# The RWKV scan of a hybrid backbone, laid out by parity of the channel tile: 64x64 products on four TensorE quadrants, key products a chunk further ahead

## The chip, the cores and the metric

The kernel runs on one core of one Trainium2 chip. The metric is device time in microseconds, the median of several runs. TensorE (PE) multiplies, with the stationary operand loaded first (PEld); VectorE (DVE), ScalarE (ACT) and GpSimd (POOL) move and combine data; SyncE (SP) issues DMAs. The TensorE array has 128 input partitions and 128 output columns. A product with 64 of each uses one quadrant of it, given by where its operands lie (partitions 0 to 63 or 64 to 127) and where its result goes.

## The reference

Two layers over 256 context and 512 latent tokens of width 1024. Each layer is FFN, token mixing, FFN. Half of the mixing is a gated DeltaNet with 4 heads, half RWKV-7 with 8 heads of 64 channels. The part that the change touches:

```
def rwkv7_scan(r, w, k, v, kk, a, state):
    def step(s, inp):
        r_t, w_t, k_t, v_t, kk_t, a_t = inp
        sa = jnp.einsum('bhvk,bhk->bhv', s, kk_t)
        s = s * w_t[:, :, None, :] - sa[..., None] * (kk_t * a_t)[:, :, None, :] + v_t[..., None] * k_t[:, :, None, :]
        return s, jnp.einsum('bhvk,bhk->bhv', s, r_t)
    xs = tuple(jnp.moveaxis(t, 1, 0) for t in (r, w, k, v, kk, a))
    state, y = lax.scan(step, state, xs)
    return jnp.moveaxis(y, 0, 1), state
```

The scan runs in both directions and the outputs are summed. The context is scanned first, and the latent scan starts from its final state.

## The kernel before

All matrices are float32 in SBUF. Phases follow one another with all engines meeting at the end of each (`end_phase`): FFN, projections, DeltaNet scan, RWKV features, RWKV scan (`pe_rw`, `act_rw`, `dve_rw`, `pool_rw`), output projection, FFN. The order of work on each engine is written out by hand, with semaphores between the engines.

The RWKV scan is done in 12 chunks of 64 tokens, for 8 heads and 2 directions ("ways", g = 0 and 1) at once, so a chunk has 16 independent 64x64 problems. Two heads share a channel tile: one head on partitions 0 to 63, the other on 64 to 127, and the four tiles (u) lie side by side. Within a chunk the recurrence is a unit lower triangular system. Its inverse X is built in six levels: X starts from blocks of two (lower0, line 2770, plus the identity, line 2773), and each level l from 1 to 5 does

- `turn_x` (L2583): X is transposed, four 128x128 transposes, and ACT moves it to Y_LEVEL (L2663),
- `lower_times_x` (L2562): the lower matrix times X, sixteen 64x32 products, masked by DVE (`mask_tx`, L2739),
- `x_times_lower` (L2572): sixteen 64x32 products, subtracted from X by DVE (`sub_xd`, L2749).

These products already use all four quadrants (`HEADS`). The others, `times` (L2462) with `keys_on_b`, `b_on_keys`, `k_on_keys`, `new_values` and the turns of K, B, V and of X's last level, further `state_on_keys` (L2486, L2487), `state` (L2503, L2504) and `output` (L2512 to L2514), take operands on partitions p and leave their result on the same partitions p: `PS[p, bank_, ...]` from `lhs(u)[p], rhs(u)[p]`. Those are the two diagonal quadrants.

While the inverse of chunk d = c+1 is built, the products of chunk c (new values, state, output) stand between the levels in PE's queue. `keys_on_b(d+1)` stands in the last level of d, `b_on_keys` at the head of the next step. POOL copies each chunk's inputs into double buffers (five copies of 128x256 for each way, L2444 to L2448) once the output of the chunk before the previous one is done. On DVE, ACT and POOL the chunks run in hardware loops (`rw_walk`, `Fori`), on PE they are written out.

Of the kernel before, what the change touches and what calls it, by code (L numbers as in the profile page):

```python
# [10 lines left out]
P = 128  # L11
# [24 lines left out]
def build(nc, x, c, ctx, c_ctx, ada_w, ada_b, norm_g, ffn_w13, ffn_w2, w_in, dn_conv, dn_a_log, dn_dt_bias,  # L36
# [3 lines left out]
    with es:  # L40
# [1567 lines left out]
        XS = 6 * (LEVELS_DN - 1) + RW_CHUNKS * LEVELS_RW  # L1608
        XTS, TS = XS, XS - RW_CHUNKS
# [31 lines left out]
        def y_count(layer, c):  # L1641
            return (XTS + Y_MORE) * layer + 1 + LEVELS_DN * c
# [6 lines left out]
        def pool_dn(pool, layer):  # L1649
# [5 lines left out]
            def step(first, a, w, i, last_used):  # L1655
# [8 lines left out]
                for g in range(2):  # L1664
# [14 lines left out]
                    used(q_decayed[g], it)  # L1679
# [17 lines left out]
                for g in range(2):  # L1697
# [3 lines left out]
                    pool.wait_ge(q_built[g], it + 1)  # L1701
                    used(o_summed[g], it)
                    gp.tensor_tensor(QE[g], QD[g], EB[g], ALU.mult).then_inc(q_decayed[g], 1)
                    pool.wait_ge(phase_done, 4)
                    pool.wait_ge(vtok_moved[g], it + 1)
# [19 lines left out]
        def pe_dn(pe, layer):  # L1725

            def spread_gates(it):
                for g in range(2):
                    pe.wait_ge(ug_built[g], it + 1)
# [14 lines left out]
            spread_gates(STEPS * layer)  # L1744
            for first, steps, a, w in dn_loops(layer):
                for i in range(steps):
                    it, own = STEPS * layer + first + i, 6 * layer + first + i
                    for g in range(2):
                        pe.wait_ge(k_built[g], it + 1)
                        product(4 * g + 1, KTc[g], KTc[g]).then_inc(kk_ready[g], 1)  # L1750
                    for g in range(2):
                        pe.wait_ge(v_built[g], it + 1)
                        pe.wait_ge(eb_ready[g], own + 1)
                        pe.wait_ge(dd_ready[g], it + 1)
                        turn(4 * g, VT[g]).then_inc(vtok_ready[g], 1)
                    for g in range(2):
                        pe.wait_ge(s_updated[g], it + 2 * layer + 1)
                        pe.wait_ge(q_built[g], it + 1)
# [7 lines left out]
                    for g in range(2):  # L1766
                        pe.wait_ge(a_ready[g], it + 1)
                        pe.wait_ge(vtok_moved[g], it + 1)
# [18 lines left out]
                    def lower_times_x(g, l):  # L1787
                        pe.wait_ge(x_ready[g], xs + l)
                        if l == 1:
                            pe.wait_ge(at_moved[g], it + 1)  # L1790
# [37 lines left out]
                    for g in range(2):  # L1828
                        pe.wait_ge(kst_ready[g], own + 1)
                        pe.wait_ge(q_decayed[g], it + 1)  # L1830
# [7 lines left out]
                    if first + i < 5:  # L1838
                        spread_gates(it + 1)
# [4 lines left out]
                    for g in range(2):  # L1844
                        pe.wait_ge(vn_ready[g], it + 1)
# [7 lines left out]
        def act_dn(act, layer):  # L1853
            sc = nc.scalar
            n = LEVELS_DN - 1
            def decays(own, it=None):
                for g in range(2):
                    act.wait_ge(gc_spread[g], own + 1)
                    if it is not None:
                        act.wait_ge(s_scaled[g], it)  # L1860
                        act.wait_ge(q_decayed[g], it)
                    sc.activation(EB[g], bank(4 * g), ACT.Exp).then_inc(eb_ready[g], 1)

            def step(first, a, w, i, last):
# [11 lines left out]
                    for g in range(2):  # L1876
                        act.wait_ge(at_turned[g], it + 1)
                        sc.activation(AT[g], bank(4 * g), ACT.Copy).then_inc(at_moved[g], 1)
                    for l in range(n):
                        for g in range(2):  # L1880
                            act.wait_ge(x_turned[g], XTS * layer + n * (first + i) + l + 1)
                            if l > 0:
                                act.wait_ge(xd_summed[g], TS * layer + n * (first + i) + l)
# [7 lines left out]
                    for g in range(2):  # L1891
                        act.wait_ge(xd_summed[g], TS * layer + n * (first + i) + n)
                        sc.activation(Y[g][lo, :, hi], blocks(4 * g + 2, lo), ACT.Copy).then_inc(y_ready[g], 1)
                    if not last:
                        decays(own + 1, it + 1)
# [7 lines left out]
        def dve_dn(dve, layer):  # L1903
# [6 lines left out]
            def distances(g, c):  # L1910
# [5 lines left out]
                dve.wait_ge(dd_ready[g], it + 1)  # L1916
# [3 lines left out]
            def step(first, a, w, i, last):  # L1920
                    it, own = STEPS * layer + first + i, 6 * layer + first + i
                    for g in range(2):
# [3 lines left out]
                        dve.wait_ge(a_ready[g], it + 1)  # L1926
# [1272 lines left out]
```

## Time and profile before

| | us |
|---|---|
| median of 3 runs (lowest, highest) | 4307.28 (4305.92, 4309.15) |
| span of the profiled execution | 4315.7 |
| PE busy | 3969.0 |
| DVE busy | 2303.0 |
| ACT busy | 1506.5 |
| POOL busy | 608.5 |

The page gives the profiled execution by its span, from first to last instruction, and no other time for it; it is 8.4 us above the median of the runs. Busy times are the union of an engine's instructions. A PE record starts where the operation was issued to the array and ends when its result is out, so records overlap, and the rate of a group is read from its length less one record's, divided by the number of records less one. A float32 product of this kernel is two MATMUL records; a transpose is one.

### The profile page before, as it was taken

To read this page: it belongs to the slowest core of one execution; us is meant where nothing else is said; L and a number is where in the kernel's file an instruction comes from. 1 tells how busy PE (TensorE), PEld (TensorE's weight loads), DVE (VectorE), ACT (ScalarE), POOL (GpSimd) and SP (SyncE) were. 2 spreads that over 40 slices of the span, in tenths; PEclk is the share of its full clock that TensorE was granted. 3 is DMA by queue.
4 is the path that set the end of the run, shared out by engine and by line. 5 is a ranking of instruction groups with operands and counts; after the bars stand their busy time and mean duration, and the time that the engine had idled before them with its cause. 6 is when DMAs were issued, how large, how long until landed. Compare 5 with 4: busy or idle time off the path is not lost. (4 is left out here: it accounts for less than half of the span.)

```text
span 4315.7 us, 99791 instructions
## 1 busy us (share of the span) xinstructions
PE 3969.0 (92%) x42373; PEld 3464.9 (80%) x42373; DVE 2303.0 (53%) x4098; ACT 1506.5 (35%) x2718; POOL 608.5 (14%) x755
## 2 busy tenths in 40 slices
PE   6999989898959998999998999989899869989998
PEld 5899977787838886899997999968787658867886
DVE  4655556464474444765556555554564463444434
ACT  4333343343253332433334333343332443333222
POOL 1222210232001100221211222100430011100000
PEclk9999999999969999999999999999999879999999
DMA  5433332000200002233223333331002000022332
GB/s 203 131 117 98 105 101 54 26 2 16 66 1 4 4 30 77 88 95 98 78 71 108 107 104 109 100 93 40 17 2 71 10 2 4 4 75 78 98 106 70
DMA packets 409058, 287.53 MB, mean 67 GB/s; under 512 B 13439, under 2 KB 366181, under 8 KB 408165
## 3 DMA queue, kind: packets, MB, share of 16 engines
q1 hardware_dynamic: 408676, 281.86, 21.4%
q8 instruction: 311, 5.10, 0.5%
q14 instruction: 71, 0.57, 0.0%
HBM read 270.27 MB, written 11.53 MB: 65 GB/s over the span
## 5 line engine op out<-in xcount | busy, mean ns | idle before, releaser
L793 ACT ACTIVATE w_hi<-w_raw 128x512 fp32r<-128x512 f32 (+1 forms) x724 | 405.2, 612 | 649.8 <-POOL w_raw L777 347.3
L800 DVE TENSOR_TENSOR w_lo<-w_raw,w_hi 128x512 fp32r<-128x512 f32 (+1 forms) x724 | 486.0, 711 | 170.2 <-ACT w_hi L793 170.2
L908 PE MATMUL PS<-x_hi,w_hi 128*128 128x384 f32 x1680 | 562.5, 335 | 0.6 <-DVE hid_flat L1089 0.4
L908 PE MATMUL PS<-x_lo,w_hi 128*128 128x384 f32 x1680 | 561.3, 334 | 0.0
L908 PE MATMUL PS<-x_hi,w_lo 128*128 128x384 f32 x1680 | 561.2, 334 | 0.0
L1174 DVE SCALAR_TENSOR_TENSOR arena<-PS,mod,arena 128x256 f32<-128x256 f32 (+1 forms) x336 | 198.2, 631 | 341.6 <-PE PS L921 341.5
L1089 DVE TENSOR_TENSOR hid_flat<-hid_flat,PS 128x384 f32<-128x384 f32 (+1 forms) x454 | 245.8, 556 | 246.5 <-PE PS L908 153.3
L921 PE MATMUL PS<-hidden_hi,w_hi 128*128 128x256 f32 (+1 forms) x1232 | 342.8, 348 | 8.5 <-DVE hidden_lo L1141 5.7
L921 PE MATMUL PS<-hidden_hi,w_lo 128*128 128x256 f32 (+1 forms) x1232 | 338.2, 344 | 0.0
L921 PE MATMUL PS<-hidden_lo,w_hi 128*128 128x256 f32 (+1 forms) x1232 | 336.9, 343 | 0.0
L908 PEld LDWEIGHTS PS<-x_hi,w_hi 128*128 128x128 f32 x1680 | 315.4, 188 | 1.2 <-DVE hid_flat L1089 1.2
L908 PEld LDWEIGHTS PS<-x_lo,w_hi 128*128 128x128 f32 x1680 | 315.4, 188 | 0.2
L908 PEld LDWEIGHTS PS<-x_hi,w_lo 128*128 128x128 f32 x1680 | 315.3, 188 | 0.0
L921 PEld LDWEIGHTS PS<-hidden_hi,w_hi 128*128 128x128 f32 x1232 | 228.2, 188 | 66.1 <-issue 31.8
L770 POOL TENSOR_TENSOR w_raw<-w_raw 128x512 f32<-128x512 f32 x60 | 84.6, 1409 | 1287.5 <-DMA w_raw<-in_ffn_w_dram 1202.5
L921 PEld LDWEIGHTS PS<-hidden_lo,w_hi 128*128 128x128 f32 x1232 | 231.6, 188 | 29.4
L921 PEld LDWEIGHTS PS<-hidden_hi,w_lo 128*128 128x128 f32 x1232 | 231.4, 188 | 29.2
L1740 PEld LDWEIGHTS PS<-arena 128*128 128x128 f32 x1344 | 156.3, 192 | 25.4 <-DVE arena L1971 9.8
L1740 PE MATMUL PS<-arena 128*128 128x128 f32 x1344 | 163.1, 279 | 12.2 <-DVE arena L1971 7.4
L2462 PE MATMUL PS<-arena 64*64 64x128 f32 (+1 forms) x3072 | 161.7, 250 | 8.7 <-POOL arena L2445 5.4
L1272 PE MATMUL PS<-p_hi,pw_hi 128*128 128x256 f32 (+1 forms) x544 | 145.9, 351 | 14.9 <-DVE p_lo L552 12.0
L2462 PEld LDWEIGHTS PS<-arena 64*64 64x64 f32 x3072 | 143.7, 137 | 14.6 <-issue 13.0
(360 smaller groups left out, 8143.9 us busy)
## 6 DMA issues: line engine op xcount, KB each, us to landing
w_raw<-in_ffn_w_dram SPq DMA_DIRECT2D x512, 256.0 KB, 4.0
arena<-in_ada_w_dram SPq DMA_DIRECT2D x120, 512.0 KB, 5.8
arena<-in_w_in_dram SPq DMA_DIRECT2D x64, 512.0 KB, 3.9
arena<-in_ada_w_dram SPq DMA_DIRECT2D x6, 2048.0 KB, 14.6
arena<-in_w_out_dram SPq DMA_DIRECT2D x16, 512.0 KB, 4.2
h_save<-arena SPq DMA_DIRECT2D x16, 384.0 KB, 3.3
arena<-h_save SPq DMA_DIRECT2D x2, 3072.0 KB, 14.8
w_raw<-in_ffn_w_dram SPq DMA_DIRECT2D x32, 128.0 KB, 2.3
```

The costliest lines, as they stand in the source:

```text
L770: v.tensor_tensor(w[:, BOTH, :], w[:, DIFF, :], w[:, UP1, :], ALU.add).then_inc(weights_summed, 1)
L793: nc.scalar.activation(w_hi[:, high_place(n, what, j), 0:size], w_raw[:, load_of[what] % 2, place, 0:size], ACT.Copy).then_inc(w_high_read ...
L800: nc.vector.tensor_tensor(w_lo[:, b, place, 0:size], w_raw[:, b, place, 0:size], w_hi[:, high_place(n, what, j), 0:size].bitcast(F32), ALU ...
L908: mm = pe.matmul(PS[:, 4 * b + bank, 0:half], w[wo], x_split[xo][:, j, k, 0:half], start=(k == 0 and q == 0), stop=(k == KH - 1 and q == 2))
L921: mm = pe.matmul(PS[:, 2 * (k % 2) + s, 0:wd], w[wo], hid_split[xo][:, f, a0:a0 + wd], start=(f == 0 and q == 0), stop=(f == tiles - 1 and ...
L1089: v.tensor_tensor(out, x, y, op).then_inc(combined, 1)
L1174: ins = v.scalar_tensor_tensor(h[:, k, a0:a0 + w], PS[:, 2 * (k % 2) + s, 0:w], mod[:, c, at:at + 1], h[:, k, a0:a0 + w], ALU.mult, ALU.add)
L1272: mm = pe.matmul(PS[:, bank_ + s, 0:w], pw[wo][:, b, k * P:(k + 1) * P], x[xo][:, k, a:a + w], start=(k == 0 and q == 0), stop=(k == KT - ...
L1740: mm = pe.matmul(PS[:, b, u * P:(u + 1) * P], lhs[:, u, :], rhs[:, u, :], start=start and (stop or u == 0), stop=stop and (start or u == D ...
L2462: mm = pe.matmul(PS[p, bank_, at + u * width:at + (u + 1) * width], lhs(u)[p], rhs(u)[p], start=True, stop=True)
```

## The change

The 16 problems of a chunk are named by v (way g and half w) and the parity e of their channel tile; p is the half of the partitions. Everything that is indexed by token (X, the masked key products, the turned K, B and V, the values) is stored by tile parity on the partitions, so that parity e decides the partitions of a token-indexed matrix and p that of a channel-indexed one. A product that goes from one kind to the other then has its operands on partitions p and its result on those of e, or the reverse: `QUADRANTS` walks all four. Products whose operands and result are both indexed by channel on the same side (`keys_on_state`, `state_on_r`) stay on the diagonal.

Further:

- K, B and V are turned by whole 128x128 transposes of two tiles (`turn_pairs`), also the last level of X.
- DVE and ACT work on both ways or both banks at once: one mask of 128x256 a level in place of two of 128x128, moves of 128x512 in place of two of 128x256. A packed copy of the level masks is made at the scan's start.
- `state_on_keys` becomes `weigh_values` and `keys_on_state`; `output` becomes `state_on_r` and `values_on_r`, and both ways go together.
- `keys_on_b` and `b_on_keys` of chunk d+1 stand in levels 4 and 5 of chunk d, and X has two buffers, so `start_x`, `add_identity` and the masks of B's products for d+1 are done before the step of d+1 begins.
- The chunks are written out on all engines, without hardware loops. The last chunk skips the state update.
- The DeltaNet scan gets other semaphore counts for the semaphores that both scans use; its instructions and their order stay.

```
-            def times(bank_, at, width, lhs, rhs):
-                for u in range(NB):
-                    for p in HALVES:
-                        mm = pe.matmul(PS[p, bank_, at + u * width:at + (u + 1) * width], lhs(u)[p], rhs(u)[p],
+            QUADRANTS = [(e, p) for e in range(2) for p in range(2)]
+            def channel_tile(v, e):
+                return 2 * (v % 2) + e
+            def keys_on_b(d):
+                pe.wait_ge(rw_copied, copied + COPIES * d + 4)
+                if d > 0:
+                    pe.wait_ge(k_moved, n0 + d)
+                    pe.wait_ge(b_moved, n0 + d)
+                for v, g, w in WAYS_HEADS:
+                    for e, p in QUADRANTS:
+                        rows, u = HALVES[p], channel_tile(v, e)
+                        mm = pe.matmul(PS[HALVES[e], KEYS_BANKS[p], v * D:(v + 1) * D], KKR[d % 2][g][rows, u, 0:D],
+                                       B_C[d % 2][g][rows, u, :], start=True, stop=True)
+                mm.then_inc(a_summed, 1)
...
+            def turn_pairs(bank_, src):
+                for v, g, w in WAYS_HEADS:
+                    pair = src[g][:, 2 * w:2 * w + 2, :].rearrange("p u t -> p (u t)")
+                    mm = pe.transpose(PS[:, bank_, v * P:(v + 1) * P], pair, ident[:, :])
...
+            def weigh_values(d):
+                pe.wait_ge(v_moved, n0 + d + 1)
+                pe.wait_ge(kr_masked, n0 + d + 1)
+                if d > 0:
+                    pe.wait_ge(rw_out_moved, RW_CHUNKS * layer + d)
...
+            def keys_on_state(d):
+                pe.wait_ge(values_weighed, n0 + d + 1)
+                if d > 0:
+                    pe.wait_ge(st_decayed, (MASKS_MADE + RW_CHUNKS - 1) * layer + MASKS_MADE + d)
+                for v, g, w in WAYS_HEADS:
+                    for e, p in QUADRANTS:
+                        rows = HALVES[p]
+                        mm = pe.matmul(PS[rows, STATE_BANKS[e], v * D:(v + 1) * D], KKR[d % 2][g][rows, channel_tile(v, e), 0:D],
+                                       ST[d % 2][rows, e, v, :], start=False, stop=(v == NB - 1))
...
+            def state(c):
...
+                for v, g, w in WAYS_HEADS:
+                    for m in range(2):
+                        for p, e in QUADRANTS:
+                            rows = HALVES[e]
+                            values = VTK[c % 2][rows, v, p * D:(p + 1) * D] if m == 0 else U_T[rows, p, v, :]
+                            mm = pe.matmul(PS[HALVES[p], STATE_BANKS[e], v * D:(v + 1) * D],
+                                           KBT[c % 2][rows, m, v, p * D:(p + 1) * D], values, start=(m == 0), stop=(m == 1))
...
+            for c in range(RW_CHUNKS):
...
+                if c >= 2:
+                    pool.wait_ge(r_on_state, rw_counts(layer)[0] + c - 1)
...
+            def start_x(d):
+                dve.wait_ge(a_summed, n0 + d + 1)
+                v.tensor_tensor(X_PAIRS[d % 2].rearrange("p v u t -> p u v t"),
+                                bank_pair(KEYS_BANKS, NB * D).rearrange("p u (v t) -> p u v t", v=NB),
+                                lower0.unsqueeze(1).unsqueeze(1).broadcast_to([P, 2, NB, D]), ALU.mult).then_inc(x0_masked, 1)
...
+            def mask_t(d, l):
+                dve.wait_ge(rt_summed, levels + (LEVELS_RW - 1) * d + l)
+                v.tensor_tensor(T_LEVEL, bank_pair(LOWER_BANKS, NB * 32).rearrange("p e (v j) -> p e v j", v=NB),
+                                level_packed[:, l - 1, :].unsqueeze(1).unsqueeze(1).broadcast_to([P, 2, NB, 32]),
+                                ALU.mult).then_inc(rt_masked, 1)
```

On PE, the turns of K, B and V of a chunk stand in levels 3 and 4 before (L2462 from id_c is a small turn, L2583 the transposes of X, L2562 and L2572 the two products of a level):

```order
L2572 MATMUL PS<-arena 64x32 x16
L2462 MATMUL PS<-id_c,arena 64x64 x16
L2583 MATMUL PS<-ident,arena 128x128 x4
L2562 MATMUL PS<-arena 64x32 x16
L2462 MATMUL PS<-id_c,arena 64x64 x16
L2572 MATMUL PS<-arena 64x32 x16
L2462 MATMUL PS<-id_c,arena 64x64 x16
L2583 MATMUL PS<-ident,arena 128x128 x4
```

The same place in a step of the changed kernel and what follows to the step's end (L2512 turns V, then K and B; L2532 turns X; L2542 and L2552 are the level's products, L2610 state_on_r, L2622 values_on_r, L2485 keys_on_b, L2564 weigh_values, L2494 b_on_keys, L2575 keys_on_state):

```order
L2512 MATMUL PS<-ident,arena 128x128 x4
L2532 MATMUL PS<-ident,arena 128x128 x4
L2542 MATMUL PS<-arena 64x32 x16
L2610 MATMUL PS<-arena 64x64 x16
L2552 MATMUL PS<-arena 64x32 x16
L2512 MATMUL PS<-ident,arena 128x128 x8
L2532 MATMUL PS<-ident,arena 128x128 x4
L2542 MATMUL PS<-arena 64x32 x16
L2622 MATMUL PS<-arena 64x64 x32
L2552 MATMUL PS<-arena 64x32 x16
L2485 MATMUL PS<-arena 64x64 x16
L2532 MATMUL PS<-ident,arena 128x128 x4
```

Three groups of 16 small turns became 12 transposes, and the products of the old chunk stand alone between the two products of a level.

On DVE, the first half of a chunk in the changed kernel (L2756 masks the key products, L2769 is mask_t, L2777 the subtraction from X, L2783 and L2791 the state):

```order
L2756 TENSOR_TENSOR arena<-PS,arena 128x512 x2
L2769 TENSOR_TENSOR arena<-PS,arena 128x256
L2777 TENSOR_TENSOR arena<-arena,PS 128x4x16x2 x2
L2756 TENSOR_TENSOR arena<-PS,arena 128x512
L2769 TENSOR_TENSOR arena<-PS,arena 128x256
L2756 TENSOR_TENSOR arena<-PS,arena 128x512
L2777 TENSOR_TENSOR arena<-arena,PS 128x4x8x4 x2
L2783 TENSOR_TENSOR arena<-arena,PS 128x512
```

Before, it stood so:

```order
L2732 TENSOR_TENSOR arena<-PS,arena 128x512 x2
L2738 ISA
L2739 TENSOR_TENSOR arena<-PS,level 128x128 x2
L2755 REGISTER_ALU
L2757 TENSOR_TENSOR arena<-arena,PS 128x256 x2
L2745 REGISTER_ALU
L2749 TENSOR_TENSOR arena<-arena,PS 128x4x16x2 x2
L2732 TENSOR_TENSOR arena<-PS,arena 128x512
```

The pair of masks of a level is one instruction now, the state's sum moved behind the second level, and the loop's register work is gone.

## Rows read from the trace of the kernel before

**Rows 1.** Page, parts 1 and 2: busy us (share) xcount; 40 slices, tenths.
```profile
PE 3969.0 (92%) x42373; PEld 3464.9 (80%) x42373; DVE 2303.0 (53%) x4098; ACT 1506.5 (35%) x2718; POOL 608.5 (14%) x755
...
PEclk9999999999969999999999999999999879999999
```
**Rows 2.** Busy time by stretch: window, length, engines' busy us (x), PEclk, DMA, GB/s.
```profile
1276.00:1286.00 10.00, 2.62 (x4) 1.17 (x4) 9.90 (x16) 0.00 (x0) 0.00 (x0) 0.62 0.00 0
...
1289.00:1297.00 8.00, 7.10 (x100) 6.30 (x100) 3.82 (x9) 0.66 (x2) 6.31 (x18) 0.59 0.01 3
1297.00:1309.00 12.00, 9.91 (x343) 8.86 (x345) 4.54 (x16) 3.16 (x8) 0.00 (x0) 1.00 0.02 4
1320.00:1600.00 280.00, 270.69 (x8796) 251.33 (x8795) 113.40 (x343) 88.62 (x235) 35.43 (x100) 1.00 0.02 4
1289.00:1609.00 320.00, 306.92 (x9839) 284.89 (x9840) 128.60 (x385) 99.44 (x263) 41.74 (x118) 0.99 0.02 4
3503.30:3825.30 322.00, 305.41 (x9839) 283.89 (x9840) 128.35 (x385) 99.42 (x263) 41.76 (x118) 0.99 0.02 4
```
**Rows 3.** Waits from 1320 to 1600: who waited for whom, us in total, times, longest.
```profile
DVE arena L2739 <- PE PS L2562: 63.5, 54, 2.4
...
PE PS L2572 <- issue: 4.4, 8, 0.8
PE PS L2462 <- issue: 2.9, 8, 0.6
PE PS L2487 <- issue: 1.5, 3, 0.6
```
**Rows 4.** Timeline of PE, two chunks' first transposes: start us, us, instruction.
```profile
1504.18 0.66 PE L2583 MATMUL PS<-ident,arena 128*128 128x128 f32 x4
...
1530.08 0.66 PE L2583 MATMUL PS<-ident,arena 128*128 128x128 f32 x4
```
**Rows 5.** Timeline of all engines in the first chunk, layer 0.
```profile
1290.57 4.53 PE L2462 MATMUL PS<-arena 64*64 64x64 f32 x48 [0.45 <-POOL arena L2444]
...
1295.03 0.85 PE L2583 MATMUL PS<-ident,arena 128*128 128x128 f32 x4
...
1299.59 0.67 PE L2562 MATMUL PS<-arena 64*64 64x32 f32 x32
...
1300.31 0.49 DVE L2739 TENSOR_TENSOR arena<-PS,level 128x128 f32<-128x128 f32 x2 [0.51 <-PE PS L2562]
...
1301.05 0.67 PE L2572 MATMUL PS<-arena 64*64 64x32 f32 x32 [0.80 <-DVE arena L2739]
...
1301.51 1.11 PE L2462 MATMUL PS<-arena 64*64 64x128 f32 x16
1301.86 0.48 DVE L2749 TENSOR_TENSOR arena<-arena,PS 128x128 f32<-128x128 f32 x2 [1.06 <-PE PS L2572]
...
1302.55 0.66 PE L2583 MATMUL PS<-ident,arena 128*128 128x128 f32 x4
...
1307.24 1.14 PE L2462 MATMUL PS<-id_c,arena 64*64 64x64 f32 x32
```
**Rows 6.** Groups by line, 1320 to 1600, shapes apart: xcount, busy us, mean ns.
```profile
L2732 DVE TENSOR_TENSOR arena<-PS,arena 128x512 f32<-128x512 f32 x42 | 29.0, 691 | 20.1 <-PE PS L2462 20.1
...
L2671 ACT ACTIVATE arena<-PS 128x512 f32<-128x512 f32 x22 | 13.1, 597 | 21.2 <-PE PS L2462 21.2
...
L2770 DVE TENSOR_TENSOR arena<-PS,arena 128x256 f32<-128x256 f32 x20 | 8.5, 424 | 12.3 <-PE PS L2462 11.5
```
**Rows 7.** Timeline of PE, DeltaNet scan of layer 0: one quadrant alone.
```profile
921.11 1.14 PE L1836 MATMUL PS<-arena 64*64 64x64 f32 x16
```
**Rows 8.** Timelines: POOL's copies; DVE beside POOL, then alone.
```profile
1288.36 0.40 POOL L2445 COPY arena<-arena 128x256 f32 x1
...
1288.70 0.40 POOL L2446 COPY arena<-arena 128x256 f32 x1
...
1292.07 1.26 DVE L2773 TENSOR_TENSOR arena<-arena,id_c 128x256 f32<-128x256 f32 x2
...
1500.45 0.75 DVE L2773 TENSOR_TENSOR arena<-arena,id_c 128x256 f32<-128x256 f32 x2
```

More of the change, by code:

```diff
@@ L2421, in rw_walk, with by_parity @@
[L2421 to L2430 removed]
+        def by_parity(start, *dims):
+            n = 1
+            for d in dims:
+                n *= d
+            return [region(start + q * n, *dims) for q in range(2)]
@@ new lines, in build, with rw_counts, bank_pair @@
+        keys_summed, r_on_state = ks_ready
+        r_moved, u_moved = r_ready
+        u_summed, out_summed = vn_summed
+        st_summed, st_added = s_summed
+        MASKS_MADE = 2
+        def rw_counts(layer):
+            chunks = STEPS * layer + 6
+            turns, levels = XTS * layer + XS, TS * layer + XS
+            states = (6 + RW_CHUNKS - 1) * layer + 6
+            return chunks, turns, levels, states
+        def bank_pair(banks, width):
+            return PS[:, banks[0]:banks[1] + 1, 0:width]
@@ new lines, in move_r @@
+            def move_r(d):
+                act.wait_ge(keys_summed, n0 + d + 1)
+                sc.activation(R_T.rearrange("p e v t -> p e (v t)"), bank_pair(STATE_BANKS, NB * D), ACT.Copy,
+                              scale=-1.0).then_inc(r_moved, 1)
+            for c, d in rw_steps():
+                if d is not None:
+                    move_y(d, 0)
+                if c is not None:
+                    move_u(c)
+                if d is not None:
+                    move_y(d, 1)
+                    move_v(d)
+                    move_y(d, 2)
+                    move_kb(d, 0)
+                    move_y(d, 3)
+                    move_kb(d, 1)
+                if c is not None:
+                    move_out(c)
+                if d is not None:
+                    move_y(d, 4)
+                    move_r(d)
+                    move_y(d, 5)
@@ L2708, in dve_rw @@
         def dve_rw(dve, layer):
             v = nc.vector
+            n0, turns, levels, states = rw_counts(layer)
+            decayed = (MASKS_MADE + RW_CHUNKS - 1) * layer
             for p in HALVES:
@@ new lines, in dve_rw @@
+            mask_br(0, 0)
+            mask_br(0, 1)
+            for c, d in rw_steps():
+                if d is None:
+                    continue
+                following = d + 1 < RW_CHUNKS
+                mask_t(d, 1)
+                sub_x(d, 1)
+                mask_kr(d, 0)
+                mask_t(d, 2)
+                mask_kr(d, 1)
+                sub_x(d, 2)
+                if c is not None:
+                    add_state(c)
+                mask_t(d, 3)
+                if c is not None:
+                    decay_state(c, 0)
+                sub_x(d, 3)
+                if c is not None:
+                    decay_state(c, 1)
+                mask_t(d, 4)
+                sub_x(d, 4)
+                if following:
+                    start_x(d + 1)
+                mask_t(d, 5)
+                if following:
+                    add_identity(d + 1)
+                sub_x(d, 5)
+                if following:
+                    mask_br(d + 1, 0)
+                    mask_br(d + 1, 1)
```

634 lines of the change are left out of this document (274 added, 360 removed).

## Prediction, made before the changed kernel ran

> **What bounds the kernel now.** I read the page first. TensorE (PE) is busy 92% of 4315.7 us and almost always at the full clock [rows 1], so only time taken off PE, or off what PE waits for, counts. The change touches the RWKV scan, once in each of two layers. Its stretches come next: 320.0 us in layer 0 (first L2462 at 1289.0, last L2514 at 1609.0) and 322.0 us in layer 1 (3503.3 to 3825.3) [rows 2]. In the steady part, 1320 to 1600, PE is busy 270.69 of 280.00 us, DVE 113.40, ACT 88.62 and POOL 35.43 [rows 2]. The waits of that window show the same: DVE waits long for PE (63.5 us at L2739), and PE's longest idle times, 4.4 + 2.9 + 1.5 = 8.8 us, have no releaser but "issue" [rows 3]. So the scan is bound by PE's own queue. From the transposes of one chunk (1504.18) to those of the next (1530.08) it takes 25.90 us [rows 4]; the 8.8 us are 0.82 us of each.
>
> The reader is to see how fast PE takes small products. A product is two records. Where all products stand on the diagonal quadrants (partitions p in, partitions p out), 32 records of 64x64 take (1.14 - 0.22)/31 = 29.7 ns each and 16 of 64x128 take (1.11 - 0.27)/15 = 56 ns [rows 5, 6]. The 64x32 products of the inversion already go to four quadrants: (0.67 - 0.22)/31 = 14.5 ns [rows 5]. On a single quadrant, 64x64 records take (1.14 - 0.22)/15 = 61 ns [rows 7]. One quadrant accepts a record each 58 to 61 ns, and its neighbours run beside it: two give 30, four give 14.5. Four whole transposes take 0.66 us, a record each (0.66 - 0.27)/3 = 0.13 us, and the next piece starts 0.59 us after them [rows 5].
>
> **What goes from PE.** Per chunk the program has 420 PE instructions before, 372 after. I name pieces by function and take 14.5 ns for a 64x64 record on four quadrants, 28 ns for 64x128 (half of 56).
> - keys_on_b, new_values: 32 records each, 0.95 to 0.46 us. state: 64 records, 1.90 to 0.93.
> - b_on_keys, k_on_keys: 32 records of 64x128 each, 1.8 to 0.9.
> - The 48 small turns of K, B and V (96 records, 2.85 us) become 12 whole transposes (1.54); the 16 small turns of X's last level (0.95) become four (0.51).
> - Output, 96 records, 2.85: state_on_r stays on the diagonal (ST and KKR lie on the same partitions as the result), 0.95; values_on_r is 64 on four, 0.93. State on keys, 64 records, 1.90: keys_on_state stays diagonal, 0.95; weigh_values 0.46.
> - The 10 pieces of 64x32 stay at 0.46.
>
> After: 36 transposes 4.6, ten pieces 4.6, three of 0.46, two of 0.93, two of 0.9, two of 0.95, and five changes from small products to transposes and back, each about 0.13 + 0.07 (0.59 less four times 0.13): 17.1 us. PE alone no longer sets the period; the chain of the inversion does, so I lay the queue out against it.
>
> **What is late next.** Row times of a level in the first chunk, where little stands between: L (lower_times_x) at 1299.59, DVE's masks at 1300.31 for 0.49, X (x_times_lower) at 1301.05, DVE's subtraction at 1301.86 for 0.48, transposes at 1302.55 [rows 5]. L to X is 1.46 us; with one mask of 128x256 (0.424, as L2770 [rows 6]) in place of two it is 1.39. X to transposes is 1.50. Each half takes the longer of this and of what PE has queued in it:
> - Level 1: L to X 1.39 (queue 0.46 + new_values 0.46); X to T 1.50 (0.46 + k_on_keys 0.9 + 0.13); T to L 0.59: 3.48.
> - Level 2: 1.39 (0.46 + state 0.93); 1.50 (turn_v 0.51 behind 0.46 + 0.13); 0.59: 3.48.
> - Level 3: 1.39 (state_on_r); 0.46 + 0.13 + eight transposes of turn_kb 1.02 = 1.61; 0.59: 3.59.
> - Level 4: 1.39 (values_on_r); 1.50 (keys_on_b of the next chunk 0.46); 0.59: 3.48.
> - Level 5: 0.46 + weigh_values 0.46 + b_on_keys 0.86 = 1.79; keys_on_state makes 1.52; T 0.51: 3.82.
> - The new chunk's first transposes 0.59; then lower_times_x waits for both mask_br, which DVE does after sub_x(5): 0.72 + 0.49 + 2 x 0.69 + 0.25 after X against 2.62 in the queue: 0.2.
>
> Sum 18.6 us. To it I add 0.5 of the 0.82 us of issue idle, since fewer instructions are fetched and some of it falls where PE waits anyway: **19.1 us a chunk**.
>
> **What hides the rest.** DVE: its masks of 128x512 stay 691 ns [rows 6], add_identity is now one 128x512 between mask_t(5) and sub_x(5), with 1.4 us of room; two 128x256 of this kind take 0.75 us alone and 1.26 beside POOL's copies [rows 8]. In all about 11 us of 19. ACT: 11 moves of 128x512 at 597 ns [rows 6] and the output: 7.4 us; move_y's 0.60 lies beside the 0.59 + 1.39 from the transposes to X. POOL: chunk d+1's copies wait for state_on_r of chunk d-1. A copy starts each 0.34 us [rows 8], four take 1.4, and keys_on_b stands 3.8 us behind the end of state_on_r; behind the waiting copy stand only copies. Without that room, each late copy would cost PE 0.34 us a chunk. The five extra small copies of DVE at the scan's start (level_packed) lie before the first a_summed. The renamed semaphores in the DeltaNet scan cost nothing: no instruction moves there.
>
> **Sum per layer.** Start to the first transposes 6.4 (before 6.0, 1289.0 to 1295.03 [rows 2, 5], now with four copies ahead instead of two); first chunk's five levels 18.3; 11 x 19.1 = 210.1; last chunk without state update 4.6 (move_y, new_values, U's move, then 0.95 + 0.93 and the gaps). 239.4 us against 320.0 and 322.0: 80.6 + 82.6 = 163 us. The profiled span is 4315.7, 8.4 above the median 4307.3 of the runs; the difference is taken from the median: **4144 us**.
>
> **Bounds of what no row shows.** 64x64 on four quadrants: not under 14.5 ns (the 64x32 rate, whose weight loads are the same 64x64), not over 29.7 (no gain). 64x128: 28 to 56. I take the low ends, because the four quadrants of L2562 and L2572 overlapped, in rows that differ only in the columns streamed. Runs of 8 transposes: 0.13 each, could be 0.11. A 128x512 add: 0.7 to 1.3, hidden.
>
> **Rivals.**
> (1) Quadrants on the same input partitions share the stream. With 32 columns there was time to take turns, with 64 there is not: 29.7 and 56 ns stay. For it: no row has two column quadrants streaming 64 columns. Against: 64x32 shows no slowing at all. Price, against the layout: level 1 second half 0.46 + 1.8 + 0.13 = +0.9; state and values_on_r +0.93 each; level 5 0.46 + 0.93 + 1.8 = +1.4: +4.2 us a chunk, 22 times, and 3 us in the first and last chunks: 4239 us. Still faster, through transposes alone and the removed instructions.
> (2) A floor per record. If small records can't follow one another faster than about 25 ns once they stream 64 columns, state and values_on_r cost 1.6 instead of 0.93 and weigh_values 0.8: +0.67 + 0.67 + 0.33 = +1.7 us a chunk: 4182 us. The 14.5 ns of the rows speak against it.
> The Trainium skill ("TensorE: Matmul & The Clock Gate", section "Wait — 56ns, not 53.3ns?") says that matmuls never start closer than about 25 ns however small they are. By it the change would stop at a rate this trace's 64x32 rows already beat by a factor of 1.7; the sum goes by the rows.
> (3) Slower than before: the clock. Ahead of the scan, with PE busy 2.62 of 10.00 us, the granted clock was 0.62, in the scan's first 8 us 0.59, that is 1.2 GHz most of the time; there 48 records (16 of 64x64, 32 of 64x128) took (4.53 - 0.27)/47 = 91 ns where the full clock gives 48 [rows 2, 5]: factor 1.9. The changed scan makes PE wait more (2 of 19 us, now 0.8 of 26). Were it at 1.2 GHz throughout, 17.1 us of work would become 32.5: +8.6 us a chunk over today, 4514 us; from a share of (25.9 - 19.1)/15.4 = 0.44 of the scan on it is slower than before; at half it is 4329 us. Against it: from 1297 to 1309 PE was busy 9.91 of 12.00 us, with 0.8 us idle in each level, and the clock stood at 1.00 [rows 2, 5].
> (4) The other engines' queues come late. DVE, ACT and POOL had loops and are now written out, so they too may stall on issue; at twice PE's 0.82 us on the chain: +1.6 a chunk, 22 times: 4180 us.
> (5) Issue idle vanishes and transposes run at 0.11: 17.4 us a chunk, 4103 us.
>
> **How the numbers follow.** Forecast 4144 with own range 4105 to 4175: 0.70. Rival 1: 0.09. Rival 2: 0.08. Rival 3: 0.05. Rival 4: 0.06. Rival 5 or lower: 0.02. The range 4100 to 4225 leaves out rivals 1 and 3, part of 5 and a rest: 0.17. Less than 0.2% (9 us) can't be told from no change. Faster: all but rival 3 and a remainder for what I overlook, 0.93; same 0.02 (a clock that drops for some 0.4 of the scan); slower 0.05.
>
> **What would show it.** Right: the period from first transposes to first transposes falls to about 19; L2494 x32 takes about 1.1 us with its tail and L2598 x64 about 1.15; PE idles about 0.4 us before X of level 1 and before the transposes of levels 2 and 4; the scan takes about 240 us. Wrong: L2598 x64 at 2 us (rival 1) or 1.8 (rival 2); a granted clock under 0.9 in the scan (rival 3); PE waiting for POOL or ACT at each chunk (rival 4).

## The result and the profile after

| | before | changed |
|---|---|---|
| median, us (lowest, highest; runs) | 4308.22 (4305.92, 4312.55; 4) | 4181.76 (4175.00, 4195.46; 4) |
| ratio (95% interval) | | 0.9714 (0.9693, 0.9734) |
| span of the profiled execution, us | 4315.7 | 4173.3 |
| MATMUL records of one RWKV scan | 9840 | 8432 |
| RWKV scan of layer 0 and of layer 1, us | 320.0, 322.0 | 250.8, 252.9 |

The change takes 126 us off, where 163 were forecast. The page's lines for PE and its clock, against [rows 1]:

```profile
PE 3803.4 (91%) x39557; PEld 3288.7 (79%) x39557; DVE 2277.8 (55%) x3910; ACT 1474.6 (35%) x2502; POOL 612.4 (15%) x753
...
PEclk8999999999988999999999999999999969999999
```

Busy time by stretch, in the columns of [rows 2]. The first two are the scans of the two layers, the others steady parts of layer 0's:

```profile
1291.00:1541.80 250.80, 224.74 (x8432) 197.74 (x8432) 116.85 (x291) 83.45 (x154) 42.58 (x116) 0.99 0.02 4
3431.00:3684.00 253.00, 224.72 (x8432) 197.66 (x8432) 116.69 (x291) 83.44 (x154) 42.68 (x116) 0.99 0.02 4
1320.00:1530.00 210.00, 190.48 (x7196) 168.21 (x7194) 99.58 (x248) 71.79 (x133) 36.78 (x100) 1.00 0.02 5
1320.00:1500.00 180.00, 162.35 (x6155) 143.33 (x6157) 84.58 (x210) 61.74 (x115) 33.10 (x90) 1.00 0.02 5
```

The two scans are 69.2 and 69.1 us shorter: nearly all of the 142.4 us between the two profiled spans. (The medians are 126.5 us apart: the profiled span of before lies 7.5 us above the median in the table, that of the changed kernel 8.5 us below.) The clock is full in the scan but for its first 6 us. What differs from the forecast is in the waits of PE, from 1320 to 1530, in the columns of [rows 3]:

```profile
PE PS L2575 <- issue: 3.9, 3, 1.6
PE PS L2485 <- issue: 2.8, 2, 1.6
PE PS L2542 <- issue: 2.7, 5, 0.7
PE PS L2552 <- issue: 2.1, 4, 0.9
PE PS L2494 <- issue: 1.7, 3, 0.8
PE PS L2532 <- issue: 1.4, 2, 0.9
PE PS L2564 <- issue: 1.1, 2, 0.6
PE PS L2598 <- issue: 0.7, 2, 0.5
PE PS L2610 <- issue: 0.5, 1, 0.5
PE PS L2622 <- issue: 0.2, 1, 0.2
```

These ten rows, 17.1 us in 210, are all of PE's waits that the view lists there. Not one names another engine: PE stood for 1.7 us a chunk with nothing to wait for. The chain against which the forecast had laid its queue shows in the weight loads alone, whose rows end sooner than those of the products (same window):

```profile
PEld PS L2532 <- DVE arena L2777: 4.6, 19, 0.3
...
PEld PS L2552 <- DVE arena L2769: 1.7, 9, 0.2
...
PEld PS L2542 <- DVE arena L2756: 1.0, 6, 0.2
```

That is 7.3 us in 210, 0.7 us a chunk, in waits of 0.3 us and less. One chunk on PE shows where it stood (start us, length, line, operation, shapes, records, and in brackets idle time before):

```profile
1375.01 0.67 PE L2542 MATMUL PS<-arena 64*64 64x32 f32 x32
1375.49 0.67 PE L2585 MATMUL PS<-arena 64*64 64x64 f32 x32
1376.22 0.74 PE L2552 MATMUL PS<-arena 64*64 64x32 f32 x32
1376.78 1.10 PE L2494 MATMUL PS<-arena 64*64 64x128 f32 x32
1377.82 0.66 PE L2532 MATMUL PS<-ident,arena 128*128 128x128 f32 x4
1378.40 0.67 PE L2542 MATMUL PS<-arena 64*64 64x32 f32 x32
1378.89 1.00 PE L2598 MATMUL PS<-arena 64*64 64x64 f32 x51
1380.36 0.39 PE L2598 MATMUL PS<-arena 64*64 64x64 f32 x11 [0.46 <-issue]
...
1384.76 1.09 PE L2512 MATMUL PS<-ident,arena 128*128 128x128 f32 x8
...
1386.71 1.13 PE L2622 MATMUL PS<-arena 64*64 64x64 f32 x61
1388.03 0.33 PE L2622 MATMUL PS<-arena 64*64 64x64 f32 x3 [0.19 <-issue]
...
1390.49 0.56 PE L2564 MATMUL PS<-arena 64*64 64x64 f32 x24
1391.57 0.34 PE L2564 MATMUL PS<-arena 64*64 64x64 f32 x8 [0.52 <-issue]
1391.74 1.08 PE L2494 MATMUL PS<-arena 64*64 64x128 f32 x32
...
1395.17 0.67 PE L2542 MATMUL PS<-arena 64*64 64x32 f32 x32
```

The pauses lie inside a piece: after 51 of the 64 records of `state` (L2598), after 61 of `values_on_r` (L2622), after 24 of `weigh_values` (L2564). No semaphore is waited for there: what a piece waits for stands ahead of its first product. From the first L2542 to the last row this chunk took 20.16 us. The same in the next chunk, at `keys_on_b`, 1.64 us at once:

```profile
1408.88 0.45 PE L2485 MATMUL PS<-arena 64*64 64x64 f32 x16
1410.97 0.46 PE L2485 MATMUL PS<-arena 64*64 64x64 f32 x14 [1.64 <-issue]
```

Counted over the trace from 1320 to 1530, there are 32 such pauses inside a piece. A pause counts where two records of one line start over 0.3 us apart, less 0.06 us for the step itself. They sum to 21.4 us; this is more than the 17.1 above, since it is taken from start to start and not from the end of the last record. The distances between them, in MATMUL records of PE, are 126, 253, 381, 254, 381, 380, 126, 128, 127, 253 and so on: multiples of about 127. The trace of before has them too, at multiples of about 125, 21 pauses and 11.0 us in 280. The view of DMA queues gives what else comes in that rhythm, for the window 1320 to 1530 (packets, MB, share):

```profile
q8 instruction: 57, 0.93, 1.8%
```

The queue that carries instructions brought 57 packets of 16 KB while PE ran 7196 records, 126 for each packet. That made the theory to test.

### The profile page after: what moved, and what is told of

Read it like the earlier page. It is cut to its first block and busy times, and to the rows that moved or that the text cites. A ratio compares the mean times of both kernels' runs of the same rounds, so it can differ in the third digit from the quotient of the medians.

```text
span 4173.3 us, 91768 instructions
## 1 busy us (share of the span) xinstructions
PE 3803.4 (91%) x39557; PEld 3288.7 (79%) x39557; DVE 2277.8 (55%) x3910; ACT 1474.6 (35%) x2502; POOL 612.4 (15%) x753
## 5 line engine op out<-in xcount | busy, mean ns | idle before, releaser
L1740 PE MATMUL PS<-arena 128*128 128x128 f32 x1344 | 164.2, 280 | 11.4 <-DVE arena L1971 7.4
L1272 PE MATMUL PS<-p_hi,pw_rw_hi 128*128 128x256 f32 x480 | 126.2, 345 | 17.0 <-DVE pw_rw_lo L1265 17.0
L864 PE MATMUL PS<-x_hi,w_hi 128*128 128x512 f32 x352 | 137.9, 392 | 3.5 <-DVE x_lo L843 3.3
```

Of the source, the lines that this page charges most:

```text
L864: mm = pe.matmul(PS[:, 4 * b + 2 * g, 0:SEQ], w[wo], lone_x(xo)[:, k, :], start=(first_k and q == 0), stop=(last_k and q == 2))
L1272: mm = pe.matmul(PS[:, bank_ + s, 0:w], pw[wo][:, b, k * P:(k + 1) * P], x[xo][:, k, a:a + w], start=(k == 0 and q == 0), stop=(k == KT - ...
L1740: mm = pe.matmul(PS[:, b, u * P:(u + 1) * P], lhs[:, u, :], rhs[:, u, :], start=start and (stop or u == 0), stop=stop and (start or u == D ...
```

## The experiments

**Theory S (supply).** PE's instructions arrive in blocks of about 127 matmul records, a block each 3.7 us or so. The scan is now bound by the number of records, whatever they do: 180/6155 = 29.2 ns each. **Rival C (chain).** The waits through the other engines, or late semaphores between them, set the period, and the profile calls them "issue" for want of a releaser. Further candidates were the rate of the array (A) and the parts of the change themselves. A steady chunk has 708 records now (the scan's last chunk has no state update, so the mean of the twelve is 703): 708 x 29.2 = 20.7 us. Before it had 820: 23.9 us, under the 25.9 that it took [rows 4].

Each run carries its own ratio to before; before was run beside e1 to e4 (median 4309.41 us), beside e5 to e8 (4311.43) and beside e9 and e10 (4312.42). The changed kernel was run again in the first and the third of these groups; e6 and e7 are held against it by way of before.

**The changed kernel again**, unedited.

> The changed kernel once more, as the measure for the other three. Theory S (instruction supply): PE's instructions arrive in blocks of about 127 matmul records; where PE runs through a block faster than the next one comes it stands still in the middle of a piece. It expects the idle times inside pieces of one line again at distances of about 127 records or multiples, about 2 us of them in a chunk of 20.5 us, and a wider spread from run to run than the kernel before has. Theory C (chain): what is over the forecast 19.1 us comes from a semaphore that DVE, ACT or POOL gives too late; it expects the idle times at the first record of pieces. Time about 4182 us by both.

Measured: 4186.87 us, ratio 0.9719 (0.9706, 0.9732); scans 254.1 and 257.8 us. From 1320 to 1500 its trace has 29 pauses inside a piece, 21.3 us, again at distances of 126 to 128 records or multiples of that. Beside e9 (e10):

> The changed kernel beside e9 on the same chip: 4180 to 4190 us.

Measured: 4192.56, ratio 0.9723 (0.9709, 0.9738), a little over the expected range. The wider spread that theory S expected isn't shown: beside each other, e1's runs spread over 4178.2 to 4189.1 us and before's over 4302.5 to 4315.1; over all its runs the changed kernel lies within 22 us (4175.0 to 4197.0), before within 16.3 (4300.3 to 4316.6).

Part of the spread is the clock at the scan's start. In the profiles of the changed kernel and of e1 the granted clock rose from 0.50 to 1.00 about 6 us after the scan's first product; in e10's, its slowest run (4196.96 us), only 27 us after it in layer 0, though PE was busy 23.05 of these 27.00 us. From that first product to the first `new_values` it took 31.4 us there, and 23.5 and 23.6 in the other two.

**More records, less work in each** (e2): the twelve whole transposes of K, B and V become 48 small products on all quadrants, as fast as small products go. They go to other banks of PSUM, so ACT's moves read both banks at once and the move of K waits for the turn of B as well.

```
-                    pair = src[g][:, 2 * w:2 * w + 2, :].rearrange("p u t -> p (u t)")
-                    mm = pe.transpose(PS[:, bank_, v * P:(v + 1) * P], pair, ident[:, :])
+                    for e, p in QUADRANTS:
+                        at = bank_ * NB * D + v * D
+                        mm = pe.matmul(PS[HALVES[e], KEYS_BANKS[p], at:at + D], src[g][HALVES[p], 2 * w + e, :],
+                                       id_c[HALVES[p]], start=True, stop=True)
```

> The 12 whole transposes that turn K, B and V of a chunk are undone: 48 small products on four quadrants instead, 96 records where there were 12, same result. On the array the pieces take 0.46 + 0.93 us instead of 0.51 + 1.02, and two changes between small products and transposes go, so theory C expects 0 to 0.2 us less a chunk, 4177 to 4182 us in all. Theory S expects 84 more records, two thirds of a block a chunk, at up to 3.5 us a block where the supply binds all the time and about half of that where it binds part of the time: +1.2 to +2.3 us a chunk, 4208 to 4233 us.

**Fewer records** (e3): `state` and `values_on_r` leave out their first sum of two (K with V in the state, V with the masked keys in the output), 64 records a chunk. The result is not that of the reference.

```
-                    for m in range(2):
+                    for m in (1,):
```

> Leaves out part of the work: the products of K with V in the state's sum and of V with the masked keys in the output (m = 0 of both), 64 records less a chunk. Both pieces stand between lower_times_x and x_times_lower, where the chain over DVE needs 1.39 us and PE's queue held 0.46 + 0.93. Theory C expects no gain, under 0.1 us a chunk, 4178 to 4184 us. Theory S expects half a block less a chunk: 0.9 to 1.8 us less, 4142 to 4162 us.

**More records where PE would wait** (e4): `keys_on_b` (from the second chunk on) and `new_values` are issued twice, 64 records a chunk, in the gaps of the inversion's chain.

```
-                for v, g, w in WAYS_HEADS:
+                for v, g, w in WAYS_HEADS * 2:
```

> keys_on_b and new_values are issued twice each (the second writes the same values again): 64 records more a chunk, put where PE waits. new_values then fills the 1.39 us of level 1 (3 x 0.46), keys_on_b the 1.50 us of level 4 (3 x 0.46 + 0.13). Theory C expects under 0.1 us a chunk, 4182 to 4185 us. Theory S expects half a block more a chunk, +0.9 to +1.8 us, 4202 to 4222 us.

| | records a scan | a steady chunk | median, us | ratio (95%) | against e1 | steady period, us | ns a record |
|---|---|---|---|---|---|---|---|
| e3 | 7696 | 644 | 4144.26 | 0.9625 (0.9612, 0.9639) | -43 | 18.81 | 29.2 |
| e1 | 8432 | 708 | 4186.87 | 0.9719 (0.9706, 0.9732) | | 20.76 | 29.3 |
| e4 | 9168 | 772 | 4221.13 | 0.9805 (0.9790, 0.9821) | +34 | 22.78 | 29.5 |
| e2 | 9440 | 792 | 4244.60 | 0.9851 (0.9837, 0.9864) | +58 | 22.88 | 28.9 |

The steady period is the mean of ten chunks in layer 0, from the start of one `new_values` to that of the next.

The windows from 1320 to 1500 of e2, of e3 and of e4:

```profile
1320.00:1500.00 180.00, 149.61 (x6192) 133.46 (x6188) 75.55 (x188) 54.56 (x102) 29.60 (x80) 0.98 0.02 5
```
```profile
1320.00:1500.00 180.00, 168.47 (x6197) 147.61 (x6200) 91.94 (x227) 67.60 (x126) 35.00 (x96) 1.00 0.02 5
```
```profile
1320.00:1500.00 180.00, 156.74 (x6121) 140.47 (x6118) 76.63 (x191) 55.88 (x104) 29.45 (x80) 0.99 0.02 5
```

The reader is to read the x behind PE's time: 6192, 6197 and 6121 records in the same 180 us, and 6155 in the changed kernel. PE was busy for 149.61 to 168.47 us, and DVE got 188 to 227 instructions done, but the number of records stayed within 1.3%. It is the one quantity that the edits don't move. From e3 to e2 the time rises by 100.3 us for 2 x 1744 records, 28.8 ns each. In e4, where the queue had been laid out with room beside the chain, the extra work still cost 34.3 us / 1472 = 23 ns a record. Were the chain the bound, e4 would have cost little, and e3, which shortens no link, would have gained little. So C fails and S holds. S missed one size: e2 came out above the 4208 to 4233 us that it had given, because it had allowed for a supply that binds part of the time only; e3 and e4 fell inside their ranges. In e2 PE's issue waits are 28.8 us in 180, the two largest sums at the small turns (L2513) and at `lower_times_x` (L2544 here):

```profile
PE PS L2513 <- issue: 5.8, 5, 1.9
PE PS L2544 <- issue: 5.0, 8, 1.1
```

In e3 they are 8.8 us in 180, no line's sum over 2.9:

```profile
PE PS L2575 <- issue: 2.9, 3, 1.1
PE PS L2564 <- issue: 2.6, 3, 1.0
```

**The supply by itself** (e5): `new_values` of chunk 5 is issued 32 times, 1024 records that wait for nothing.

```
-                for v, g, w in WAYS_HEADS:
+                for v, g, w in WAYS_HEADS * (32 if c == 5 else 1):
```

> The supply by itself: new_values of chunk 5 is issued 32 times in a row in each layer (it writes the same values each time), 1024 records of 64x64 on four quadrants with no wait between them. If only the array counts, they take 14.5 ns each, 14.9 us, as inside the pieces. Theory S: after what is already on the chip is used up they come at the supply's pace, a block of 127 records each 3.5 to 3.7 us, 28 to 29 ns a record, some 27 to 29 us in all, in bursts of 127 records with a pause behind each.

Measured: 4242.98 us, from a single run. PE's timeline there:

```profile
1414.38 0.77 PE L2585 MATMUL PS<-arena 64*64 64x64 f32 x35
1415.30 2.09 PE L2585 MATMUL PS<-arena 64*64 64x64 f32 x128 [0.15 <-issue]
1419.04 2.09 PE L2585 MATMUL PS<-arena 64*64 64x64 f32 x128 [1.65 <-issue]
1422.79 2.09 PE L2585 MATMUL PS<-arena 64*64 64x64 f32 x128 [1.65 <-issue]
1426.26 2.09 PE L2585 MATMUL PS<-arena 64*64 64x64 f32 x128 [1.38 <-issue]
1430.28 2.09 PE L2585 MATMUL PS<-arena 64*64 64x64 f32 x128 [1.93 <-issue]
1434.02 2.09 PE L2585 MATMUL PS<-arena 64*64 64x64 f32 x128 [1.65 <-issue]
1437.77 2.09 PE L2585 MATMUL PS<-arena 64*64 64x64 f32 x128 [1.65 <-issue]
1441.24 1.56 PE L2585 MATMUL PS<-arena 64*64 64x64 f32 x91 [1.38 <-issue]
```

This is the mechanism laid bare. 128 records run in 2.09 us, (2.09 - 0.22)/127 = 14.7 ns each, then PE stands for 1.4 to 1.9 us, and a block begins each (1437.77 - 1415.30)/6 = 3.75 us: 29.3 ns a record. The array needs a little over half of the time in which its instructions come. Two layers with 992 extra records each at 29.3 ns are 58 us, which puts the kernel at 4240 from its median of 4182.

The trace also holds when each packet of the instruction queue q8 started and how long it took, and that ties the pauses to the supply. From 1415 to 1442 the packets started at 1416.46, 1420.11, 1423.84, 1427.37, 1431.40, 1435.17 and 1438.96, each 1.05 to 1.19 us after a block's first record; they took 0.93 to 1.44 us, and the next block began 1.23 to 1.49 us after each had ended. These three parts make up the 3.5 to 4.0 us of a block, and the longest packet (1.44 us, from 1427.37) stands in the longest block (1426.26 to 1430.28), the shortest ones (0.93 and 0.96) in the shortest. The scans show the same: all 32 pauses of the changed kernel from 1320 to 1530 and all 21 of before from 1320 to 1600 end 1.20 to 1.60 us after a packet of q8 has ended.

**The quadrants of one piece** (e6): `values_on_r` puts its result on the diagonal quadrants, so its products read and write the same half. This changes what is computed: half of its products are added to other rows of the output than theirs. Count and order of records are the same.

```
-                            mm = pe.matmul(PS[HALVES[p], STATE_BANKS[e], v * D:(v + 1) * D], values, weights,
+                            mm = pe.matmul(PS[HALVES[e], STATE_BANKS[p], v * D:(v + 1) * D], values, weights,
```

> Leaves the result wrong in part: the 64 records of values_on_r go to the two diagonal quadrants, as before the change, with the same number of records; all else as changed. The piece takes 1.86 us on the array in place of 0.93 and stands in a gap of 1.39. Array and chain alone: +0.93 us a chunk, +20 us, 4206 us. Theory S (records, not the array, set the pace): most of it is hidden under the supply, 0 to 0.3 us a chunk, 4187 to 4194 us. So what the four quadrants bring by themselves would be small.

Measured: 4196.23, ratio 0.9741 (0.9728, 0.9754): about 0.2%, or 9 us, above the changed kernel's 0.9719, with the intervals just touching, and a little over the expected 4187 to 4194 us. The trace can't tell it from nothing: e6's steady periods of the two layers, 21.01 and 20.92 us, lie within those of the unedited kernel (20.55 and 20.79, in e1 20.76 and 21.22, in e10 20.98 and 21.23). The piece itself doubled, from 61 records in 1.13 us to (timeline of e6):

```profile
1410.28 1.91 PE L2622 MATMUL PS<-arena 64*64 64x64 f32 x59
```

(1.91 - 0.22)/58 = 29.1 ns a record. That is 0.9 us a chunk of array time, 22 us in 24 chunks, of which less than half came through. The rest fell into time in which PE would have waited for instructions anyway.

**The look-ahead undone** (e7): the products `keys_on_b` and `b_on_keys` of a chunk, and what DVE makes of them, go back to the head of the chunk's own step.

```
                 if d is not None:
+                    if d > 0:
+                        keys_on_b(d)
+                        b_on_keys(d)
                     turn_x(d, 0)
...
                     x_times_lower(d, 4)
-                    if following:
-                        keys_on_b(d + 1)
```

> Undoes the look-ahead: keys_on_b, b_on_keys, start_x, add_identity and mask_br of a chunk stand at the head of its own step, with the same records. The chain gets longer: keys_on_b 0.46, its end and start_x 1.2, b_on_keys 0.86, its end and two masks 1.9 before lower_times_x, about 4.4 us where 0.8 are there now, less 0.4 in level 5: the chain alone makes 22 us a chunk. With the same 703 records theory S has 20.2 as the other bound, and PE catches up on instructions while it waits, so 22 to 23 us a chunk and +33 to +50 us: 4220 to 4237 us. If it costs over 3 us a chunk (4250 us), supply and chain add instead of the longer one deciding.

Measured: 4222.20, ratio 0.9807 (0.9787, 0.9828), 38 us above the changed kernel by the ratios. Its waits of PE from 1320 to 1530:

```profile
PE PS L2494 <- DVE arena L2744: 9.0, 10, 0.9
PE PS L2542 <- DVE arena L2755: 7.3, 9, 0.8
PE PS L2532 <- DVE arena L2776: 6.0, 10, 0.6
PE PS L2552 <- issue: 2.5, 6, 0.9
```

Here the chain decides: 22.3 us of waits for DVE, nine or ten of each kind. And issue fell from 17.1 to 6.3 us: the next block lands while PE waits for DVE. The instruction queue stands idle too at times: its packets start up to 6.29 us apart here, at most 4.15 in the changed kernel's window. PE ran 5749 records from 1320 to 1500, where e1 ran 6133: 31 ns each, not the supply's pace any more.

**Before without hardware loops** (e8): on DVE, ACT and POOL the loops of the scan are written out, nothing else.

```
-                with eng.Fori(0, pairs) as i:
+                for i in range(pairs):
```

> The kernel before, with the chunks of DVE, ACT and POOL written out and no hardware loops. Theory S: 98% of the blocks fetched in the scan are PE's, so neither the written-out programs nor the loops' register work matter: 4300 to 4312 us. If the written-out programs take supply from PE, it gets slower by 5 us or more.

Measured: 4310.05, ratio 0.9998 (0.9988, 1.0007). Loops or none on the other engines, no difference in the time.

**A version that needs fewer records** (e9). The first products of a chunk's inverse, `keys_on_b`, can be had from those of `b_on_keys`: the entries on one side of a pair of tokens, moved by one row. DVE picks them from the other product's result with a mask, and one product with a shifted identity moves them down. That is 30 records a chunk fewer, and nothing is left out.

```
-            def keys_on_b(d):
...
+            def shift_first(d):
+                pe.wait_ge(x0_masked, n0 + d + 1)
+                pe.wait_ge(br_masked, n0 + d + 1)
+                pe.matmul(PS[:, KEYS_BANKS[0], 0:NB * D], down_one[:, :], first_odd.rearrange("p u v j -> p (u v j)"),
+                          start=True, stop=True).then_inc(a_summed, 1)
```

> A version with fewer records and the same result. keys_on_b served only to start X, which takes one element in two rows from it. Those elements are in b_on_keys's result too, transposed: DVE masks them (128x256), one product with a shift matrix puts them a partition further (two records of 256 columns), DVE adds the identity. 32 records become 2, 673 a chunk in place of 703; the chain gets no shorter, PE may wait 0.4 us for the start of X. Theory S at 29.2 ns a record: 0.9 us less a chunk, 4163 to 4170 us. Theory C: no change or up to +0.4 us a chunk, 4187 to 4196 us.

Measured: 4174.81, ratio 0.9688 (0.9673, 0.9702), beside e10's 0.9723 (0.9709, 0.9738) on the same chip: 18 us faster than the changed kernel by the medians, 15 by the ratios. 720 records fewer at 29.2 ns are 21 us, and theory S had 4163 to 4170 us. The steady period fell as it said, by 0.9 us: 20.07 and 20.25 us in the two layers, beside e10's 20.98 and 21.23. Some of the rest was lost at the start: in e9's profile the granted clock stayed at 0.50 for the first 13 and 12 us of its scans, and the first `new_values` came 27.2 and 26.8 us after the start, against 23.5 in the changed kernel. Its window from 1320 to 1500:

```profile
1320.00:1500.00 180.00, 168.15 (x6097) 145.44 (x6094) 85.11 (x225) 64.10 (x117) 33.09 (x90) 1.00 0.02 5
```

Of the versions that leave nothing out this is the fastest. PE is busier than in the changed kernel (168.15 against 162.35 us) and the chunk shorter: what it saved is instructions.

## Why the prediction was right or wrong

**What bounds the kernel before**: right in the main. The array's queue set the period and the supply bound of 23.9 us lay below it, though pauses of the supply already took 1.0 us of each chunk (11.0 us in 280). The 25.90 us are one chunk; the mean of ten in layer 0 is 26.28.

**Rates of the array**: right. Inside a piece, 64x64 records on four quadrants take (1.13 - 0.22)/60 = 15 ns (L2622; forecast 14.5), 64x128 take (1.08 - 0.27)/31 = 26 ns (L2494; forecast 28), and the run of eight transposes 0.12 us each (L2512; forecast 0.13). So rival 1 (a shared stream) is out: L2622 x61 took 1.13 us, not 2. Rival 2 (a floor of 25 ns a record) is out as a rule of the array, though its time, 4182, is the one measured. The mechanism is another: records do follow at 15 ns, and are short of supply for as long again.

The Trainium skill ("TensorE: Matmul & The Clock Gate", section "Wait — 56ns, not 53.3ns?") has a floor of about 25 ns from start to start. The blocks of e5 at 14.7 ns within a block don't agree; only the mean over blocks, 29.3 ns, lies in its neighbourhood.

**The chain**: right in its sizes and places, wrong as the bound. From `lower_times_x` to `x_times_lower` of level 1 it took 1376.22 - 1375.01 = 1.21 us (forecast 1.39), from the transposes to L2542 of level 2 0.58 (0.59). The forecast had PE idle before X of level 1 and before the transposes of levels 2 and 4. The weight loads do wait for DVE once a chunk before the first and twice a chunk before the others (L2552 and L2532 above), but for 0.2 to 0.3 us and not 0.4. The halves of levels with a pause in them are longer. With the look-ahead in place the chain asks for less than the supply takes anyway; e7 shows that it becomes the bound when the look-ahead goes.

**The step that failed**: "To it I add 0.5 of the 0.82 us of issue idle, since fewer instructions are fetched and some of it falls where PE waits anyway". Measured, issue idle is 1.7 us a chunk, not 0.5. The step took the idle time as a share of the number of instructions, when it was the difference between the time in which a block of them runs and the time in which the next arrives. Twice the pace in the array made each block run out sooner. The period was 20.55 us in layer 0 (ten steady chunks) and 20.79 in layer 1, against 19.1. The start, the first and the last chunk took 45.3 and 45.0 us, 48.4 forecast, so luck hid some 3 us a layer of the miss. Together that is 11.4 and 13.5 us more than forecast for the two layers. The other 13 between 4144 and 4182 come with the run that was profiled, the shortest of its four: its two scans took 503.7 us, those of e1's profile 511.9, those of e10's 522.3. With 4182 us the kernel lies outside the 4105 to 4175 that the forecast held most likely, and inside its wide range only.

The rows for it were there: [rows 3] put PE's idle time down to issue and to nothing else, in 19 places, none over 0.8 us, and 820 records in 25.9 us are 31.6 ns each. The prediction looked for no rhythm in them.

**Rival 3** (the clock) is out as the main cause: 0.99 over both scans of the changed kernel, 1.00 in their steady parts. It isn't nothing: beside the late rise in e10 and e9, the profiles of e1, e2, e4, e5, e7 and e10 show it at 0.50 for a few us inside a scan, and that of before doesn't. **Rival 4** (other engines' queues late) is out: what PE's weight loads wait for DVE is 0.7 us a chunk, at places where the forecast's chain had it wait, and e8 is at 0.9998. **Rival 5** (issue idle vanishes) is the opposite of what came.

**The parts of the change**, by what undoing them costs: whole transposes 58 us (e2), through 84 records a chunk; the look-ahead 35 to 38 us (e7); the quadrants of `values_on_r` 9 us at most (e6); loops nothing (e8). They don't add up, since each is measured with the others in place. What all quadrants together gave wasn't tried. By the prediction's own prices, an estimate: three pieces at 0.49 us more, two at 0.97 and two at 0.9 would add 5.2 us to the array's 17.1 a chunk, and 22.3 us would stand over the supply's 20.7.

## What to carry to other kernels

Count the matmul records in a stretch of written-out TensorE code and divide its length by them. Where that gave 29 to 30 ns here, the stretch was bound by the supply of instructions, and neither a faster array nor work moved into gaps helped, only fewer records (wide transposes, products joined, results reused); at 31 to 32 ns (e7, before) something else was. A hardware loop on PE, which might need fewer blocks, wasn't tried. Pauses that the profile puts down to "issue" and that fall inside a piece, at distances of about 127 records, are its sign. A change that makes the array faster should be laid against this bound as well as against the chain of waits.

## What the runs showed of the hardware

- A block of 16 KB of PE's instructions holds 126 to 128 of this kernel's matmul records and comes each 3.75 us when PE does nothing but wait for them (e5); from 1320 to 1500 in the changed kernel, e1 to e4, e9 and e10 each 3.7 to 3.8 in the mean. The instruction queue's packets took only 1.8% of the DMA engines' time from 1320 to 1530. In e5 a block's time is 1.05 to 1.19 us until the next packet starts, 0.93 to 1.44 for the packet, and 1.23 to 1.49 until its first product runs. Why the next packet doesn't start sooner is open; no run changed it.
- The Trainium skill ("Runtime: NRT & Kernel Launch", section "Instruction fetch mechanics") says that instructions come in blocks of 16 KiB, 256 of them, on the engine's own DMA queue. This trace agrees: the packets of q8 have 16 KB each, and at two instructions a record (a weight load and a matmul, the profile's page counts x39557 of each) 256 instructions are the 128 records of a block in e5. The section also says that the cost of crossing a block is mostly hidden, because the sequencer issues more slowly than blocks come in. Here it is not: 1.65 us of pause after 2.09 us of work (e5).
- What the supply lacks isn't lost when PE waits for something else: with 22.3 us of waits for DVE, issue idle fell from 17.1 to 6.3 us (e7). The next block lands in that time.
- Four quadrants stream 64 columns of float32 each without slowing one another: 14.7 ns a record (e5) against 29.1 on the two diagonal ones (e6).
- The granted clock doesn't rise at the same place in each run of one kernel: 6 us after the scan's first product in two profiles of the changed kernel, 27 us after it in a third (e10, layer 0), where the scan's start cost 8 us more.
